# Four tiles side by side at the start of the feed-forward stages, and extra products in TensorE's waits at three seams

## The reference

```python
def second_block(x, ...):
    for layer in range(DEPTH):
        h = rmsnorm(x, norm_mix_pre[layer])
        m = retention_mixer(h, ...) if layer < N_A_LAYERS else dilated_mixer(h, ...)
        x = x + rmsnorm(m, norm_mix_post[layer])
        f = conv_ffn(rmsnorm(x, norm_ffn_pre[layer]), ffn_w_up[layer], ...)
        x = x + rmsnorm(f, norm_ffn_post[layer])
        if layer == N_A_LAYERS - 1:
            k_sh, v_sh = shared_kv(x, kv_norm, att_w_kv, pos)
    return x

def conv_ffn(h, w_up, conv_w, conv_b, w_down):
    u = h @ w_up                      # 1024 x 5632
    gate, val = u[..., :D_FF], u[..., D_FF:]
    conv = conv_b + conv_w[0..2] * shifted gate
    return (gelu(conv) * val) @ w_down
```

## Time and profile before

| what | value |
|---|---|
| median of 3 runs | 2950.25 us (2949.13 to 2950.26) |
| the profiled execution's own time | 2949.85 us |
| its span, first to last instruction | 2948.1 us |
| TensorE (PE) busy | 2913.9 us, 99% of the span |
| VectorE (DVE), ScalarE (ACT), GpSimd (POOL) busy | 1730.9, 1056.2, 1276.4 us |
| mean granted TensorE clock | 0.995 of full speed |
| chain that ended last | PE 95%, DVE 3%, ACT 1%, issue 1% |

### The profile page before, as it was taken

The page is one execution under the profiler, slowest core; times in us unless marked ns, Lnnn a source line. Parts: engine busy times, 40 slices in busy tenths (PEclk is TensorE's granted clock), DMA queues, the critical chain, the costliest instruction groups (busy, mean ns, idle before and its releaser), DMA issues.

```text
span 2948.1 us, 38963 instructions
## 1 busy us (share of the span) xinstructions
PE 2913.9 (99%) x15210; PEld 2364.0 (80%) x15210; DVE 1730.9 (59%) x3058; ACT 1056.2 (36%) x1826; POOL 1276.4 (43%) x926
## 2 busy tenths in 40 slices
PE   8999999999999999999999999999999999999999
PEld 6787778877777788888888788887888888788888
DVE  5765554565754554655563687516666666587732
ACT  4444442354443432533332322224333333432222
POOL 4333334453333344544444455544434434355553
PEclk9999999999999999999999999999999999999999
DMA  6222223232222223322223233332222222233332
GB/s 200 86 79 72 72 79 100 86 107 72 79 72 74 85 93 93 107 80 83 81 79 93 74 106 100 94 99 89 85 74 79 73 77 75 72 89 97 97 96 79
DMA packets 79501, 260.20 MB, mean 88 GB/s; under 512 B 10878, under 2 KB 15742, under 8 KB 79320
## 3 DMA queue, kind: packets, MB, share of 16 engines
q1 hardware_dynamic: 78744, 255.63, 28.3%
q10 hardware_dynamic: 576, 2.10, 0.2%
HBM read 255.53 MB, written 6.09 MB: 89 GB/s over the span
## 4 chain that ended last, share of the span: by engine, by line
PE 95%; DVE 3%; ACT 1%; issue 1%; DMA 0%; POOL 0%; DVEq 0%; ACTq 0%
PE bank L765 25%; PE bank L767 25%; PE bank L766 25%; PE bank L987 2%; PE bank L966 1%; PE bank L944 1%; PE bank L782 1%; PE bank L942 1%; PE bank L783 1%; PE bank L789 1%; PE bank L1136 1%; PE bank L1137 1%; PE bank L1142 1%; DVE h_lo L1993 1%; PE bank L1231 1%
## 5 line engine op out<-in xcount | busy, mean ns | idle before, releaser
L607 POOL TENSOR_TENSOR w_lo<-w_raw,w_hi 128x512 fp32r<-128x512 f32 x458 | 614.2, 1341 | 1592.9 <-ACT w_hi L1371 1592.9
L1371 ACT CAST w_hi<-w_raw 128x1024 fp32r<-128x1024 f32 x458 | 480.5, 1050 | 1308.2 <-PE bank L767 1215.3
L765 PE MATMUL bank<-h_hi,w_hi 128*128 128x512 f32 x2367 | 940.6, 397 | 0.0
L767 PE MATMUL bank<-h_hi,w_lo 128*128 128x512 f32 x2367 | 923.3, 390 | 0.0
L766 PE MATMUL bank<-h_lo,w_hi 128*128 128x512 f32 x2367 | 921.6, 389 | 0.0
L609 POOL TENSOR_TENSOR w_lo<-w_raw,w_hi 128x512 fp32r<-128x512 f32 x458 | 658.9, 1439 | 35.9
L765 PEld LDWEIGHTS bank<-h_hi,w_hi 128*128 128x128 f32 x2367 | 444.7, 188 | 95.5 <-issue 6.9
L767 PEld LDWEIGHTS bank<-h_hi,w_lo 128*128 128x128 f32 x2367 | 444.2, 188 | 95.3
L766 PEld LDWEIGHTS bank<-h_lo,w_hi 128*128 128x128 f32 x2367 | 445.0, 188 | 88.0
L2323 DVE TENSOR_SCALAR m<-bank,gains 128x512 f32<-128x512 f32 x47 | 35.3, 751 | 315.9 <-ACT ta L1598 197.0
L1533 ACT ACTIVATE probs<-probs,small_columns 128x128 f32<-128x128 f32 (+2 forms) x192 | 101.9, 531 | 105.4 <-DVE small_columns L2052 98.8
(11 more groups left out here) (345 smaller groups left out, 4573.1 us busy)
## 6 DMA issues: line engine op xcount, KB each, us to landing
w_raw<-in_w SPq DMA_DIRECT2D x458, 512.0 KB, 3.5
bias_copies<-bias_vectors SPq DMA_DIRECT2D x1, 2560.0 KB, 12.4
x_res<-in_x_t ACTq DMA_DIRECT2D x4, 512.0 KB, 8.6
bias<-bias_copies SPq DMA_DIRECT2D x8, 256.0 KB, 3.5
bias<-bias_copies SPq DMA_DIRECT2D x16, 128.0 KB, 2.4
out_x<-x_res SPq DMA_DIRECT2D x16, 128.0 KB, 1.7
bias_copies<-bias_vectors SPq DMA_DIRECT2D x1, 1280.0 KB, 9.4
ple_raw<-in_p_t SPq DMA_DIRECT2D x2, 512.0 KB, 4.0
```

Of the source, the lines that this page charges most:

```text
L607: pool.tensor_tensor(WL[slot][:, 0:half], RAW[slot][:, 0:half], WH[slot][:, 0:half].bitcast(F32), ALU.subtract).then_inc(sems["lo_half"], 1)
L765: pe.matmul(banks[bank][:], WH[slot][:, w], hi[:, k, :], start=start, stop=False)
L767: pe.matmul(banks[bank][:], WL[slot][:, w], hi[:, k, :], start=False, stop=stop).then_inc(sems["kt_done"], 1)
L1371: act.copy(WH[slot][:], RAW[slot][:]).then_inc(sems["hi_done"], t.one("hi_done"))
```

## The change

- `UP_BESIDE = 4`: a feed-forward stage opens four output tiles side by side instead of three. TensorE's loop, ScalarE's `past`, VectorE's `ready` and the order of the weight stream are changed to agree. The number of tiles and of products stays.
- `meanwhile(name, bank, n)`: n products of an operand that has long been finished (128 of its columns as weights, all 512 as the moving side), into the bank that the next tile opens; nothing reads them.
- At the three seams it is called with 3 products between the two column sums in `linear`, with 3 before `spread` at the start of the next stage, and with 7 after that spread, before the first fresh product.

```diff
+UP_BESIDE = 4
...
+        BUSY, BUSY_WITH = (("ret", 0), ("ffn", 0), ("dil", 1)), (3, 3, 7)
...
+                def meanwhile(self, name, bank, n):
+
+                    x = {"ret": RH[:, KT, :], "ffn": FLO[:, 4, :], "dil": H2H[:, KT - 1, :]}[name]
+                    if bank in self.last:
+                        waited, value = self.last[bank]
+                        pe.wait_ge(sems[waited], value)
+                    for _ in range(n):
+                        pe.matmul(banks[bank][:], x[:, 0:P], x, start=True, stop=True)
...
                     self.column_sums(OUTB, TC, last=False)
+                    if (name, l) in BUSY:
+                        self.meanwhile(name, self.rot % ROTATION, BUSY_WITH[0])
                     pe.wait_ge(sems["m_squared"], t.at("m_squared"))
...
                 def ffn_up(self, l):
+                    self.meanwhile(("ret", "dil")[l], self.rot % ROTATION, BUSY_WITH[1])
                     self.spread(OUTB)
-                    self.fresh([self.rotate() for _ in range(3)], HH, HL)
-                    for x in range(3, 2 * FT):
+                    self.meanwhile(("ret", "dil")[l], self.rot % ROTATION, BUSY_WITH[2])
+                    self.fresh([self.rotate() for _ in range(UP_BESIDE)], HH, HL)
+                    for x in range(UP_BESIDE, 2 * FT):
...
+                    self.meanwhile("ffn", DIL_FIRST_BANKS[0], BUSY_WITH[1])
                     self.spread(OUTB)
+                    self.meanwhile("ffn", DIL_FIRST_BANKS[0], BUSY_WITH[2])
                     opened = [self.open(b) for b in DIL_FIRST_BANKS[0:3]]
...
-                    self.past(3, KT)
-                    self.past(1, KT)
+                    self.past(UP_BESIDE, KT)
                     root()
...
-                            self.n += 3 * KT
-                        elif tile > 2:
+                            self.n += UP_BESIDE * KT
+                        elif tile >= UP_BESIDE:
                             self.n += KT
-                        dve.wait_ge(sems["kt_done"], self.n - (2 - tile) if tile < 2 else self.n)
+                        dve.wait_ge(sems["kt_done"], self.n - max(UP_BESIDE - 1 - tile, 0))
...
-        return beside(*both[0:3]) + both[3:] + beside(down[0], down[1]) + down[2:]
+        return beside(*both[0:UP_BESIDE]) + both[UP_BESIDE:] + beside(down[0], down[1]) + down[2:]
```

## The result

The changed kernel took 2953.53 us in the median of 20 runs (2951.75 to 2956.66), the kernel before 2949.94 us in 20 runs beside it (2948.12 to 2951.73): a ratio of 1.0014 (95% interval 1.0008 to 1.002), so 3.6 us slower. That is under 0.2%, but clear of the noise and above the range given. The profiled execution of the changed kernel took 2954.99 us, its span is 2953.2 us, 5.1 more than before.

The account below looks back on a forecast made before the run. TensorE was 99% busy, but VectorE's chain was taken to pace the feed-forward stages. Terms 0.43 + 0.43 - 0.27 - 0.29 - 0.49 - 0.49 = -0.7 us gave a forecast median of 2949.5 us, range 2947.2 to 2952.4.

Parts of the forecast that it names:

- The reading of the bound: In feed-forward stages VectorE's chain sets the pace and hides the clock's cost; TensorE is busy 99% of the span.
- the wait at operand tile 7: In ffn0 TensorE catches up with the operands and waits 0.46 us; four tiles side by side would remove this.
- The gate at the squares' sums: In feed-forward stages the column sums wait 1 to 3 us for VectorE's last addition, slowed from 0.69 to 1.67 us.
- +0.43: In each feed-forward stage, us lost because the slowed last addition moves the start of the squares' sums from 1667.28 to 1667.71.
- -0.29: In ffn0, us gained at the head of VectorE's chain by a spread at full clock.
- After the gate nothing is late: In feed-forward stages, sums, four K-tiles and spread follow as before; the inverse root has slack, 3.7 us from sums to spread.
- rival (1): At the seams the clock falls despite the extra products; spreads stay slow, about +1.4, 2951.6 us; chance 0.25.
- the terms of -0.27 and -0.49: In dil, us gained: 0.27 from regained clock before a wait for low weights, 0.49 from a faster spread.
- The range: For the whole kernel's time, 2947.2 to 2952.4 us.
- all groups of products cold: At the three seams all three groups of extra products run at half clock: +2.2, 2952.4 us.
- Rival (3): TensorE alone decides and neither additions nor weights gate: 8.7 us gained, 2941.6 us; chance 0.03.

Follow-up runs that it names:

- run with products only: Changed kernel with three tiles side by side again and the extra products kept: 2949.64 us, ratio 0.9998 against the kernel before.
- The filled wait: Changed kernel with 11 more products just before TensorE's wait for the squares in each feed-forward stage: 2949.85 us, ratio 0.9999 against the kernel before.
- sums behind the fifth tile: Changed kernel with squares' column sums four K-tiles later and the spread behind K-tile 2 of the sixth tile: 2944.48 us, ratio 0.9982.
- fewer additions: Changed kernel with three of VectorE's seven additions of squares left out in each feed-forward stage: 2943.96 us, ratio 0.9981.
- run with the sums later: Changed kernel with squares' column sums at the sixth tile's K-tile 1, spread and ScalarE's root later too: 2950.09 us, ratio 1.0001.

## Why the prediction was wrong, point by point

**The reading of the bound** held: the clock of the old cold stretches was hidden by the operands in the feed-forward stages. The run with products only shows it, by the wait at operand tile 7 that grows instead.

**The gate at the squares' sums** came as worked out, its size in part by luck. From the sums of TC to the squares' sums ffn0 took 34.31 us before and 34.47 after, +0.16 us; the terms were +0.43 and -0.29. The last addition took 1.65 us (forecast 1.67) with GpSimd's gap gone. The wait there, forecast as 1 to 3 us, was 2.61. The rule of the Trainium skill, page "SBUF — State Buffer", section "Who interferes with whom", agrees in kind; taken to the letter, as the prediction estimates from it, it would have made the addition 2.0 us, which the trace does not show.

Two smaller terms were off and cancelled. The three products ahead of the spread were put at nothing; at full clock they still held it, from 3.88 us behind the sums of TC to 4.04, though the inverse root was ready 0.30 us before it (0.15 before the change):

```profile
1637.40 0.18 DVE L1869 RECIPROCAL small_columns<-small_columns 128x4 f32<-128x4 f32 x1 [0.35 <-ACT small_columns L1396]
1638.51 0.69 DVE L2019 TENSOR_TENSOR m<-m,bank 128x512 f32<-128x512 f32 x1 [0.94 <-PE bank L877]
```

So VectorE's chain began 0.13 us earlier, not 0.29. Against that, TensorE started 0.05 us after the last addition, where the prediction took 0.15.

**The step that failed** is "After the gate nothing is late: sums, four K-tiles and the spread follow as before". The wait was in the forecast, but its price was taken as its length alone. It let the clock fall to 1.2 GHz under the products behind it: from the squares' sums to the next spread 5.32 us instead of 3.67, +1.65 us in ffn0, and 5.33 instead of 3.67 in ffn1. The prediction counted cold stretches that the change would remove and never asked where a new one would begin, though it had just moved TensorE's idle time from a place where the clock did not matter to one where it did. The filled wait shows this term by itself, 3.7 us in both stages together. Two such terms, 3.3 us, added to the forecast of 2949.5 make 2952.8, against 2953.53 measured.

**ffn1** is no repeat of ffn0. Already before the change its waits were not the same: TensorE waited 1.38 us for the inverse root there, against 0.98. In the changed kernel its three products ahead of the spread ran cold in the profiled execution:

```profile
2570.73 1.62 PE L766 MATMUL bank<-h_hi 128*128 128x512 f32 x3 [0.55 <-ACTq L1420]
2572.14 1.06 PE L877 MATMUL bank<-ident,small_columns 128*128 128x128 f32 x4
```

They held the spread until 2572.14, with the inverse root there at 2571.41:

```profile
2571.23 0.18 DVE L1869 RECIPROCAL small_columns<-small_columns 128x4 f32<-128x4 f32 x1 [0.35 <-ACT small_columns L1396]
```

VectorE's chain began 0.57 us later behind the sums of TC than before, where the forecast had it 0.49 earlier, and up to the squares' sums the stage took 0.84 us more. That is the mechanism of rival (1), at its size of about 0.5 us, in one seam out of three.

**The dilated seam** gained what was said and lost it further on. TensorE waited 0.44 us for the low weights of the second operand, as forecast, and got there 0.46 us earlier from the sums of ffn0. By 2073.24 it waited 0.29 us for VectorE's eviction, and the first scores of the next pair came 70.27 us after those sums, against 70.28 before. So the terms of -0.27 and -0.49 did not reach the end of the stage in this execution, and the prediction did not follow it so far. VectorE accounts for 0.29 us of it; the rest stays open. Nor does one execution settle it: from the sums of ffn0 to those of dil it took 560.26 to 562.04 us in the eight profiled kernels with extra products, and 560.94 to 561.98 in the three without.

**The range** had its upper end at all groups of products cold, 2952.4. It held no term for the clock behind the new wait. Rival (3), where TensorE alone decides, was far off for this kernel; but of the 8.7 us it named, the kernels with the sums behind the fifth tile and with fewer additions got about two thirds (5.6 and 6.1).

## What to carry to other kernels

When a change makes the busiest engine early at a wait, price the wait and what follows it: here an idle of TensorE of 2.6 us cost 1.7 us more on the products behind it. Then move the wait's place, not only its length: twelve products ahead of the sums, work that had to be done anyway, and an earlier spread turned a loss of 3.6 us into a gain of 5.6. And test the halves of a change together and apart, since here each half alone did nothing, and both together lost until the third piece was moved.

## What the runs showed of the hardware

- The granted clock fell to 0.50 behind waits of 2.61 and 2.60 us in the middle of dense products, and stayed at 1.00 behind waits of 1.04 and 1.21 us at the same place (one profiled execution each). Eleven products that nothing reads, in a wait of that length, kept it at 1.00.
- Products put into waits keep the clock up only in part: the changed kernel still had 3.4 us at 0.50 at the seam to ffn1, and the run with products only had one such stretch at each feed-forward seam. With the same products the run with the sums later stayed at 1.00 at all three seams, and the one with fewer additions had 6.8 us at 0.50 at the dilated seam, so one execution tells little of one seam.
- The changed kernel's runs spread over 4.9 us, those of before over 3.6. Its four slowest (2955.67 to 2956.66 us) are the four with the lowest mean clock, 0.995 and 0.996 against 0.997 and 0.998. That fits falls of the clock that differ from run to run, but no run tries it.
